# The gated output of the third attention unit taken ahead of weight remainders, and the sixth modulation piece behind it

## The reference, cut to what matters

```python
proj = h @ w_in                                   # q, k, v of three branches, g_nsa, ...
o_nsa = nsa_attention(...)                        # gates * (compressed + selected + window)
y_b = (o_nsa * jax.nn.silu(g_nsa)) @ w_nsa_out    # the gated output
gm = jax.nn.sigmoid(h @ w_merge + b_merge)        # the merge gates
merged = gm[:, :, 0] * y_a + gm[:, :, 1] * y_b
...
mod = jax.nn.silu(c) @ w_ada + b_ada              # second block's modulation
```

## Time and profile before

| | us |
|---|---|
| median of 3 runs | 2280.42 (2279.46 to 2280.89) |
| the profiled execution's own time | 2282.75 |
| its span, first to last instruction | 2281.1 |
| PE busy | 2250.8 (99%) |
| DVE busy | 1556.1 (68%) |
| ACT busy | 1105.4 (48%) |
| first attention, four groups of about 86.6 us | 372 to 707 |

### The profile page before, as it was taken

How to read it: one execution, slowest core, us unless ns; L and a number is a source line. 1 busy time by engine, 2 the same in 40 slices (tenths; PEclk the granted TensorE clock), 3 DMA queues, 4 the chain that set the end, 5 groups by cost and what they waited for, 6 DMA issues and landing times.

```text
span 2281.1 us, 31278 instructions
## 1 busy us (share of the span) xinstructions
PE 2250.8 (99%) x10377; PEld 1863.9 (82%) x10377; DVE 1556.1 (68%) x1936; ACT 1105.4 (48%) x1437; POOL 149.9 (7%) x285
## 2 busy tenths in 40 slices
PE   8999999999999999999999999999999999999998
PEld 6888888788788888888888888888888888888886
DVE  5685777777776556788777776666555666655566
ACT  6454445566564444533366554445444443444444
POOL 1000110000000000011011210000000000000000
PEclk9999999999999999999999999999999999999999
DMA  8887897555665766598588886666666666666564
GB/s 286 288 283 266 302 337 253 205 193 202 211 225 175 272 209 228 199 320 292 195 284 288 311 317 248 235 217 213 210 212 221 230 222 228 227 213 208 207 205 146
DMA packets 150104, 546.49 MB, mean 240 GB/s; under 512 B 17249, under 2 KB 17392, under 8 KB 148496
## 3 DMA queue, kind: packets, MB, share of 16 engines
q1 hardware_dynamic: 112400, 406.37, 51.4%
q0 software_dynamic: 34752, 129.71, 16.3%
q10 hardware_dynamic: 2880, 9.44, 1.0%
HBM read 534.92 MB, written 10.53 MB: 239 GB/s over the span
## 4 chain that ended last, share of the span: by engine, by line
PE 87%; DVE 6%; ACT 3%; issue 2%; DMA 2%; DVEq 0%; ACTq 0%; SPq 0%
PE ps L1805 22%; PE ps L1807 22%; PE ps L1806 22%; PE ps L1922 5%; PE ps L1924 5%; PE ps L1923 5%; DVE w_lo L1065 2%; PE ps L1844 2%; DMA raw<-ws_dram 2%; ACT prob L787 1%; ACT w_hi L619 1%; PE ps L1981 1%; PE ps L2028 1%; DVE prob L1226 1%; PE ps L1822 0%
## 5 line engine op out<-in xcount | busy, mean ns | idle before, releaser
L1065 DVE TENSOR_TENSOR w_lo<-raw,w_hi 128x1024 fp32r<-128x1024 f32 x761 | 927.8, 1224 | 617.5 <-ACT w_hi L619 599.7
L619 ACT ACTIVATE w_hi<-raw 128x1024 fp32r<-128x1024 f32 x753 | 795.7, 1061 | 996.5 <-PE ps L1807 859.8
L1805 PE MATMUL ps<-w_hi,a_hi 128*128 128x512 f32 x1632 | 638.6, 391 | 3.4 <-DVE w_lo L1065 1.7
L1807 PE MATMUL ps<-w_hi,a_lo 128*128 128x512 f32 x1632 | 636.2, 390 | 0.0
L1806 PE MATMUL ps<-w_lo,a_hi 128*128 128x512 f32 x1632 | 636.0, 390 | 0.0
L1805 PEld LDWEIGHTS ps<-w_hi,a_hi 128*128 128x128 f32 x1632 | 306.9, 188 | 67.1 <-issue 2.2
L1807 PEld LDWEIGHTS ps<-w_hi,a_lo 128*128 128x128 f32 x1632 | 306.9, 188 | 64.1
L1806 PEld LDWEIGHTS ps<-w_lo,a_hi 128*128 128x128 f32 x1632 | 307.1, 188 | 63.1
L1922 PE MATMUL ps<-w_hi,a_hi 128*128 128x512 f32 x640 | 258.5, 404 | 0.4 <-DVE w_lo L1065 0.4
L1924 PE MATMUL ps<-w_hi,a_lo 128*128 128x512 f32 x640 | 249.8, 390 | 0.0
L1923 PE MATMUL ps<-w_lo,a_hi 128*128 128x512 f32 x640 | 249.3, 390 | 0.0
(11 more groups left out here) (310 smaller groups left out, 2125.4 us busy)
## 6 DMA issues: line engine op xcount, KB each, us to landing
raw<-ws_dram SPq DMA_DIRECT2D x769, 512.0 KB, 4.2
ada<-wa_dram POOLq DMA_DIRECT2D x192, 512.0 KB, 4.8
gates_spill<-gst ACTq DMA_DIRECT2D x16, 512.0 KB, 5.4
ga<-gates_spill POOLq DMA_DIRECT2D x8, 512.0 KB, 4.2
gb<-gates_spill POOLq DMA_DIRECT2D x8, 512.0 KB, 6.0
bias_c<-b_merge_dram POOLq DMA_DIRECT2D x9, 256.0 KB, 4.9
x<-x_dram SPq DMA_DIRECT2D x4, 512.0 KB, 7.6
cb<-c_dram POOLq DMA_DIRECT2D x2, 1024.0 KB, 5.1
```

The lines of the kernel that those rows point to most:

```text
L619: act.activation(w_hi[:, k.slot(RING), :], raw[:, k.slot(RING), :], ACT.Copy).then_inc(hi_done, 1)
L1065: dve.tensor_tensor(w_lo[:, k.slot(RING), :], raw[:, k.slot(RING), :], w_hi[:, k.slot(RING), :].bitcast(F32), ALU.subtract).then_inc(lo_do ...
L1805: pe.matmul(o, hi(m, tb), w_hi[:, s, cols], start=m == 0, stop=False)
L1807: mm = pe.matmul(o, lo(m, tb), w_hi[:, s, cols], start=False, stop=m == of * kts - 1)
```

## The change

The gated output of a unit becomes a function `gated`. For turns 1, 2 and 4 it is called where it was. In turn 3 it is called for unit 2 directly behind `p_ready` of unit 3, ahead of the remainders of tiles 23 and 24. The modulation piece 2 stays in turn 1; piece 5, which stood behind `p_ready` in turn 3 ahead of the remainders, now comes at the end of turn 3, behind `y_lo` of unit 2. The same instructions are executed, and only DVE's order is changed.

```diff
-                        if nsa_ and j % 2:
-                            m = 3 * (j // 2) + 2
-                            modulation(ada0 + m, m)
+                        if nsa_ and j == 1:
+                            modulation(ada0 + 2, 2)
+
+                    def gated(u, tb, h0):
+                        dve.wait_ge(a.pv_done, (u + 1 + 1).n)
+                        dve.tensor_tensor(ot[:].rearrange("p (h s) -> p h s", h=2),
+                                          ps[:, 6, 0:a.nh * P].rearrange("p (h s) -> p h s", h=a.nh),
+                                          gT[:, h0:h0 + 2, tb * P:(tb + 1) * P], ALU.mult).then_inc(a.o_ready, 1)
+
                     if nsa_:
+                        if j == nu - 1:
+                            gated(u0 + (j - 1), *a.units[j - 1])
                         fill(a.fill[2 + j])
...
                         if nsa_:
-                            dve.wait_ge(a.pv_done, (u + 1 + 1).n)
-                            gated = ot[:].rearrange("p (h s) -> p h s", h=2)
-                            dve.tensor_tensor(gated, o, gT[:, h0:h0 + 2, tb * P:(tb + 1) * P], ALU.mult)\
-                                .then_inc(a.o_ready, 1)
-                            o = gated
+                            if j != nu - 1:
+                                gated(u, tb, h0)
+                            o = ot[:].rearrange("p (h s) -> p h s", h=2)
                         dve.wait_ge(a.y_hi_done, (u + 1 + 1).n)
                         dve.tensor_tensor(lo, o, hi.bitcast(F32), ALU.subtract).then_inc(a.y_done, 1)
+                    if nsa_ and j == nu - 1:
+                        modulation(ada0 + 5, 5)
```

## The result

The changed kernel takes 2293.72 us (median of 4 runs, 2293.43 to 2296.48) against 2280.65 for the kernel before: a ratio of 1.0059, 95% interval 1.0045 to 1.0073. It is 13 us slower, where 2283.0 was predicted, with 2286.0 as the upper end. Its profiled execution took 2296.48, span 2294.8.

The account below looks back on a forecast made before the run. TensorE, 99% busy, was taken as the bound, with DVE's `q_ready` a second bound at group starts. Three groups at +1.3 and the last at -1.35 gave +2.6 us on the median: 2283.0, range 2279.3 to 2286.0.

Parts of the forecast that it names:

- Steps 1 to 3: Turn 3, DVE and ACT: earlier `gated` ends the wait on `pcT`, -1.35 us a group; the later piece loses nothing there.
- Step 4: POOL's queue: sixth `ada` load and `bias_c` wait for the later piece, so `bias_c` lands at 534.1 instead of 531.13.
- the one unknown: How long `bias_c` takes to land: 5.3 us assumed, 4.1 to 6.5 seen; each 0.1 us is 0.3 of the sum.
- Step 5: DVE waits for `bias_c` at the gate's first half, becoming 2.25 us later; TensorE waits 2.1 at tile 24.
- step 6: Next group's start: late DVE delays `q_ready` and q's transposes, making each of three groups 1.3 us longer.
- Rival B: `bias_c` lands at 6.0 us or more, for instance through descriptors held back by remainders: 2286.8 us, slower; chance 0.15.

Follow-up runs that it names:

- bias_early: Changed kernel with `bias_c` of chunk 2 loaded ahead of the fourth `ada` load, so it no longer waits for the sixth piece: 2277.43 us.
- idle_pieces: Changed kernel with pieces 3 and 4 in turn 2 and piece 5 in turn 3, while ACT takes the exponentials: 2275.48 us.
- bias_before_ada: Changed kernel with `bias_c` of chunk 2 still behind the sixth piece but issued ahead of the sixth `ada` load: 2291.93 us.
- piece_last_only: Kernel before with only the sixth piece moved, behind `y_lo` of unit 2; gated output stays behind the two remainders: 2287.6 us.
- half_weights: Changed kernel loading only the left half of each weight tile in the first attention: ratio 1.0003 to the kernel before.
- piece_between: Changed kernel with the sixth piece between the two remainders of turn 3: ratio 1.0023 to the kernel before.
- gate_then_piece: Changed kernel with the sixth piece directly behind the gated output, ahead of turn 3's remainders: 2278.98 us.

## Why the prediction was wrong

**Steps 1 to 3 were right.** `ot` comes directly behind `prob`, `pcT` is copied at 437.66, 2.2 us ahead of the transposes at 439.89, and the 1.35 us show as such: 1.37 in the last group, which has nothing against it (66.57 us from its transposes of q to its last value products, 67.94 before), and 1.4 a group in bias_early and idle_pieces.

**Step 4 had the right mechanism**: the piece holds back the sixth `ada` load, and that holds back `bias_c`. bias_early undoes just that and gives the whole gain.

**The landing, "the one unknown", was mis-sized.** I took 5.3 us "since the `ada` load stands directly ahead of it as before, and two weight loads still fall beside it". Measured: 8.0. The failed reasoning is "still". Before, the piece stood ahead of the remainders, so POOL's loads went out first, on empty engines, and the weight loads came behind them. Behind the remainders it is the other way round. The prediction's own times have it: `bias_c` at 528.8 and the `ada` load 0.7 ahead of it, at 528.1, leave the weight load of 526.0 not beside them but 2.1 us ahead of both. The kernel before's weight loads of 525 to 535 us took 4.0 to 5.6 us, so it would still be moving. The kernel before, 524 to 525.5 and 526.5 to 528 us (q0 is POOL's queue, q1 SP's; the share is of 16 engines):

```profile
DMA packets 0, 0.00 MB, mean 0 GB/s; under 512 B 0, under 2 KB 0, under 8 KB 0
...
q0 software_dynamic: 115, 0.47, 89.4%
```

The changed kernel, 440.3 to 441.5 and 443 to 445 us:

```profile
q1 hardware_dynamic: 83, 0.32, 83.5%
...
DMA packets 130, 0.49 MB, mean 246 GB/s; under 512 B 10, under 2 KB 10, under 8 KB 130
...
q1 hardware_dynamic: 70, 0.28, 39.2%
q0 software_dynamic: 60, 0.21, 34.3%
```

Before, POOL's load had the engines to itself until it was through: the weight load issued at 525.8 doesn't show in the second stretch at all. Now the weights hold them when it is issued, and afterwards the two queues move together and slower. From 443 to 449 us all loads together move at 283 GB/s (246, 358 and 246 in its three parts of 2 us), and the engines are 79% busy; in the kernel before, 440 to 446 us in the same group, it was 345 GB/s and 96%. The Trainium skill's page "DMA: Bandwidth & Descriptors", section "SWDGE vs HWDGE vs iDMA", says that each DMA engine takes turns between its queues. The shares of 39.2 and 34.3% side by side agree; in the kernel before the turns are as long as a whole load (q0 alone at 89.4%). That sentence of the page gives nothing for the drop in rate, and no run here settles where it comes from.

What the traces do show is when it happens. POOL's load begins to move 1.2 to 1.5 us behind its issue in the first group of each, before (438.5, first packets at 439.7) as after (440.4, 441.6), so it isn't held back at its start. In the changed kernel, bias_early and bias_before_ada weight packets are still moving at that moment, and the loads of POOL take 7 us or more. In piece_last_only and half_weights the weight packets have ended by then, and the `ada` load takes 3.4 to 3.8. But a weight load still moving is not enough alone. The 4.1 of the earlier trace rows, called "issued alone" in the prediction, was alone only in POOL's queue: the weight load of 531.7 moved until 536.2 beside it. There one more load was issued close behind; in the late cases it is two or three within about 2 us, and in piece_last_only it is three with nothing moving ahead, which gives 5.4. So in these traces it takes both, the load still moving and the crowd behind it. The step is not sharp: in piece_between the last weight packets end just as POOL's begin, and `bias_c` takes 7.1 to 7.5, the `ada` load 5.7 to 6.6. I had read the rows for *when* the loads went out, and not for what the engines did at that time; a view of the DMA engines around 525 us would have shown them empty.

**Step 5's wait was right in place and wrong in size** for that reason: the step from the last value products to tile 24 is 6.87 us (1.97 before), 4.9 of delay where 2.1 was predicted.

**A term was missing: the granted clock.** After waits of PE of 2.9 to 4.6 us (changed, bias_before_ada) the clock fell for 8 to 10 products, 1.4 to 2.0 us; after waits of up to 2.5 us (piece_last_only, piece_between, half_weights) it stayed at 1.00. At the predicted 2.1 it would most likely not have mattered.

**The two sizes.** By the prediction's own price, 0.3 us for each 0.1, the landing of 8.0 makes 2.5 + 8.1 = 10.6 us of the measured 14.5. The other 3.9 are the clock's: it costs 5.4 us in three groups, and 1.5 of them fall into the wait for `q_ready` that step 6 has there.

**Step 6 was right, and the size of its exception too.** In gate_then_piece, piece_last_only, piece_between and half_weights the step in front of q's transposes is 1.0 us in place of 0.4 (step 6 gives 0.9), and in piece_last_only the chain gives the periods within 0.12. In the changed kernel that second wait is absent: the fallen clock makes TensorE later than `q_ready`. The sum then is, for the first group, -1.4 + 4.9 + 1.4 = +4.9 against a measured 4.97; with the three groups' 15.8 and the last one's -1.4 it is 14.5.

**Rival B** had the sign and the place, with a landing of 6.0 us or more; I had given it 0.15 and a price of 6.4, by a mechanism (descriptors held back by remainders) that wasn't it: POOL's load begins to move as soon behind its issue as before, and half_weights, with the same remainders, lands it in 4.4 to 4.9. The range ended near the longest landing seen, 6.5, and a landing behind a moving weight load with others crowding in was not among the rows.

## What to carry to other kernels

A move on one engine reorders every queue that it releases: write down which DMAs hang on the moved instruction, what stands behind them in the issuing queue, and who waits for those. Then look at what the DMA engines do at the new moment, not only at the time of issue: the same 256 KB directly behind the same `ada` load took 3.6 us with no weight load beside, 5.3 with weight loads issued beside, and 8 with one still moving ahead as well. A load that a deadline hangs on belongs ahead of what it needn't wait for: ahead of the wait for the piece it cost nothing (bias_early), ahead of the `ada` load alone it won back a third of the loss (bias_before_ada).

## What was not expected of the hardware

`bias_c` took 7.0 to 8.0 us with nothing ahead in its own queue. A 512 KB `ada` load, 3.3 to 3.7 us nearly everywhere in the attention, took 7.1 to 7.8 behind a weight load still moving, and 8.7 to 9.8 with `bias_c` ahead as well. A shift of POOL's issue against the weight loads by about 1 us (from the changed kernel to piece_last_only) brings `bias_c` from 8.0 back to 5.4. And the six waits of TensorE of 2.9 us and more cost more than their length, by 1.4 to 2.0 us of the lower clock; the nine waits of 2.5 us and less did not.
